# Scan stage: three token shifts spread over the slots of the inverse, and X's update signalled apart from its transpose's

## What is computed

```
z  = h @ w_in                                    # projection
z  = z[t-1]*w[0] + z[t]*w[1] + z[t+1]*w[2]       # centred_shift, three taps per channel
r, k, v, decays, rates = ...                     # from z, with sigmoids, a norm of k, exponentials
step(S):  s_kk = S kk ;  S <- S diag(d) - s_kk (kk*a)^T + v k^T ;  y = S r     # forward and reverse
```

## Time and profile before

| | us |
|---|---|
| median of 3 runs | 3002.47 (3000.74 to 3004.83) |
| profiled execution, its own time | 3004.26 |
| profiled execution, span | 3002.5 |
| PE busy over the span | 2732.5 (91%) |
| DVE busy | 1182.1 (39%) |
| ACT busy | 608.2 (20%) |
| POOL busy | 250.1 (8%) |
| mean granted TensorE clock | 0.974 of full speed |

### The profile page before, as it was taken

One profiled execution on the slowest core, in us unless ns is written; L12 is line 12 of the kernel. 1 busy time (PEld: TensorE's weight loads), 2 busy tenths in 40 slices (PEclk: granted clock), 3 DMA queues, 4 the chain that ended last, 5 costly groups with the idle time before them and its releaser, 6 DMA issues. The chain is left out here.

```text
span 3002.5 us, 69531 instructions
## 1 busy us (share of the span) xinstructions
PE 2732.5 (91%) x31106; PEld 1482.5 (49%) x31106; DVE 1182.1 (39%) x2613; ACT 608.2 (20%) x1255; POOL 250.1 (8%) x282
## 2 busy tenths in 40 slices
PE   6899999999999899988998989989887999899998
PEld 3566666776664445444433433433333455455553
DVE  3565566566643673163221211212013245423333
ACT  3233233333321100010000000000002344322222
POOL 1121122112200000001000000000000021110000
PEclk9999999999999999998999999999997999999999
DMA  5000000000005773167999999999995421042210
GB/s 204 24 26 14 19 26 20 21 19 26 12 26 196 279 282 113 56 273 297 430 431 431 430 431 430 431 431 430 431 431 196 134 71 37 0 123 63 63 42 29
DMA packets 191501, 557.42 MB, mean 186 GB/s; under 512 B 32140, under 2 KB 119714, under 8 KB 166646
## 3 DMA queue, kind: packets, MB, share of 16 engines
q1 hardware_dynamic: 191222, 553.19, 47.0%
HBM read 550.65 MB, written 2.24 MB: 184 GB/s over the span
## 5 line engine op out<-in xcount | busy, mean ns | idle before, releaser
L2327 PE MATMUL bank<-arena,xe 128*64 128x512 f32 x1024 | 345.2, 601 | 35.0 <-DMA gates<-in_exp_w_dram 24.0
L684 PE MATMUL bank<-arena 128*128 128x512 f32 x384 | 201.5, 647 | 6.7 <-DVE vj L1610 5.3
L2327 PEld LDWEIGHTS bank<-arena,xe 128*64 128x64 f32 x1024 | 107.9, 138 | 183.1 <-issue 170.4
L3354 PE MATMUL bank<-arena 128*128 128x512 f32 x384 | 176.2, 607 | 3.4 <-PEq L3232 3.4
L2327 PE MATMUL bank<-arena,hidT 128*64 128x512 f32 x512 | 171.7, 599 | 2.4 <-DMA gates<-in_exp_w_dram 1.9
L2780 PE MATMUL bank<-arena 128*128 128x512 f32 x320 | 143.3, 596 | 0.0
L2327 PE MATMUL bank<-mg_ring,xe 128*64 128x512 f32 x256 | 117.9, 615 | 20.9 <-DMA u<-in_exp_w_dram 20.9
L2552 DVE TENSOR_TENSOR x<-x,bank 128x512 f32<-128x512 f32 x64 | 43.7, 686 | 227.6 <-PE bank L2365 227.6
L2545 DVE TENSOR_TENSOR hid<-hid,bank 128x512 f32<-128x512 f32 x32 | 19.8, 682 | 285.4 <-PE bank L2327 285.4
L2327 PE MATMUL bank<-ys,xe 128*64 128x512 f32 x256 | 114.5, 600 | 19.1 <-DMA arena<-in_exp_w_dram 18.5
L1548 DVE TENSOR_TENSOR pm<-bank,m_level 128x512 f32<-128x512 f32 x120 | 82.7, 689 | 118.1 <-PE bank L763 117.1
(11 more groups left out here) (530 smaller groups left out, 5471.7 us busy)
## 6 DMA issues: line engine op xcount, KB each, us to landing
arena<-in_exp_w_dram SPq DMA_DIRECT2D x96, 2048.0 KB, 26.8
gates<-in_exp_w_dram SPq DMA_DIRECT2D x24, 2048.0 KB, 29.6
ys<-in_exp_w_dram SPq DMA_DIRECT2D x24, 2048.0 KB, 26.7
mg_ring<-in_exp_w_dram SPq DMA_DIRECT2D x24, 2048.0 KB, 25.7
u<-in_exp_w_dram SPq DMA_DIRECT2D x24, 2048.0 KB, 30.2
ws_w<-in_ada_w_dram SPq DMA_DIRECT2D x40, 1024.0 KB, 5.2
arena<-in_odd_w_in_dram SPq DMA_DIRECT2D x32, 512.0 KB, 3.9
arena<-in_w_in_dram SPq DMA_DIRECT2D x24, 512.0 KB, 4.2
```

The source lines that it names most:

```text
L684: last = mm(to[:], wj[:, c, i, :], hT[:, c, 0:T], start=(c == 0), stop=(c == KT - 1))
L2327: r[e] = mm(out[a, :], lhs[j][:, a], w[:, j, 512 * c:512 * c + 512], start=(first and j == 0), stop=(last and j == len(lhs) - 1), skip_gro ...
L3354: last = mm(o[:], w[:, i, t, :], hT[:, t, :], start=(t == 0), stop=(t == KT - 1))
```

## The change

The three shifts of K_X, K_V and R_X are taken apart into taps that stand in three successive places instead of one (V_X stays whole). The first two pieces of the projection R_X move on PE from (1,3,0), ahead of `solve`, to (1,3,1), behind `read_out`. `parts(j, 11)` moves on DVE from (1,3,0), ahead of `update`, to (1,3,1), behind `state`; `parts(b, 2)` from (2,2,1) to (2,3,0). X's update gets a semaphore of its own: for l > 0 the next product waits for that and no longer for XT's update, and a wait for XT's update stands between the product and the right side (levels 1 to 3). ACT's and POOL's programs are unchanged.

```diff
             def product_ready(j, g, l):
                 if l == 0:
                     sc.settled(pe, "x0", j, g)
-                if level_no(j, g, l) > 1:
+                if l:
+                    pe.wait_ge(S["x_first"], x_first_no(j, g, l - 1))
+                elif level_no(j, g, l) > 1:
                     pe.wait_ge(S["x_done"], level_no(j, g, l) - 1)
...
-                if at == (1, 3, 0):
+                if at == (1, 3, 1):
                     project(b, R_X, 0, KT)
                     project(b, R_X, 1, KT)
-                if at == (1, 3, 1):
                     squares(b)
...
                             product(j, s, l, sj, n + l - 1 if l else None, at_step)
+                        if l < 4 and live(j) and l:
+                            pe.wait_ge(S["x_done"], level_no(j, s, l - 1))
                         if l < 4 and s < 2:
                             right_side_beside_scores(sj, n + l, j, 4 + 4 * s + l)
...
-                    tt(x, x, z(INV), ALU.subtract)
+                    tt(x, x, z(INV), ALU.subtract).then_inc(S["x_first"], 1)
...
-            def shift(j, which):
+            def shift(j, which, taps=range(3)):
...
+                mine = Steps(dve, S["shift"], (shift_no(j, which - 1) if which else SHIFTED * j) + taps[0] * len(parts_))
+                if taps[0] == 0:
+                    dve.wait_ge(S["proj"], proj_no(j, which))
...
+                for tap in taps:
+                    if tap:
+                        mine.settle()
+                    for dst, z, w, n in parts_:
+                        if tap == 0:
+                            mine.then(ts(dst, z, w[1], None, ALU.mult))
+                        elif tap == 1:
+                            mine.then(stt(dst[:, 1:n], z[:, 0:n - 1], w[0], dst[:, 1:n], ALU.mult, ALU.add))
+                        else:
+                            mine.then(stt(dst[:, 0:n - 1], z[:, 1:n], w[2], dst[:, 0:n - 1], ALU.mult, ALU.add))
+                mine.settle()
...
             def beside(j, at):
                 a, b = j - 1, j + 1
-                if at[0] < 2 and at[1] < 4 and at[2] == 0:
+                if at[0] < 2 and at[1] < 4 and at[2] == (1 if at[0:2] == (1, 3) else 0):
                     parts(j, 4 + 4 * at[0] + at[1])
...
+                if at == (0, 2, 1):
+                    shift(b, K_X, (0,))
                 if at == (0, 3, 0):
-                    shift(b, K_X)
+                    shift(b, K_X, (1,))
+                if at == (0, 3, 1):
+                    shift(b, K_X, (2,))
...
+                if at == (1, 2, 0):
+                    shift(b, K_V, (0,))
                 if at == (1, 2, 1):
-                    shift(b, K_V)
+                    shift(b, K_V, (1,))
                 if at == (1, 3, 0):
+                    shift(b, K_V, (2,))
                     gated(a)
...
                 if at == (2, 2, 1):
                     parts(b, 0)
+                    shift(b, R_X, (0, 1))
+                if at == (2, 3, 0):
+                    shift(b, R_X, (2,))
                     parts(b, 2)
-                    shift(b, R_X)
```

More of the change, by code:

```diff
@@ L524, in stage_scan @@
     names = """p_loaded a2_loaded w2_loaded wk_loaded wr_loaded wv_loaded g_loaded zeroed ones_made summed grown q_grown r_grown
-        prod mask corr x_done part_moved xt0_done r_mm r_neg u_mm u_done z_mm z_done z_scaled y_mm y_copied
+        prod mask corr x_first x_done part_moved xt0_done r_mm r_neg u_mm u_done z_mm z_done z_scaled y_mm y_copied
         proj shift par_done sq_done ss_root ss_inv inverse_wide kk_done t1_done kf_done akk_done ke_done be_done q_done
@@ L595, in stage_scan @@
         level_no = lambda j, g, l: (j * GROUPS + g) * LEVELS + l + 1
+        x_first_no = lambda j, g, l: (j * GROUPS + g) * (LEVELS - 1) + l + 1
         step_no = lambda j, n: j * STEPS + n + 1
@@ L1585, in params @@
                     ts(col(j, 18), col(j, 10), -1.0, 1.0, ALU.mult, ALU.add).then_inc(S["par_done"], 1)
-            def shift(j, which):
+            def shift(j, which, taps=range(3)):
                 if not live(j):
                     return
-                dve.wait_ge(S["proj"], proj_no(j, which))
-                mine = Steps(dve, S["shift"], shift_no(j, which - 1) if which else SHIFTED * j)
-                taps_of = lambda i: [col(j, 3 * t + i) for t in range(3)]
+                w_of = lambda i: [col(j, 3 * t + i) for t in range(3)]
@@ L1594, in shift @@
                 z_of = proj_bank(j, which)
                 if which == K_X:
-                    if j:
+                    parts_ = ((kj[:, XS], z_of[:], w_of(1), T),)
+                elif which == K_V:
+                    parts_ = ((kj[:, CS], z_of[:, 0:TC], w_of(1), TC), (vj[:, CS], z_of[:, TC:2 * TC], w_of(2), TC))
+                elif which == R_X:
+                    parts_ = ((rj[:], z_of[:], w_of(0), T),)
+                else:
+                    parts_ = ((vj[:, XS], z_of[:], w_of(2), T),)
@@ L1597, in shift @@
+                mine = Steps(dve, S["shift"], (shift_no(j, which - 1) if which else SHIFTED * j) + taps[0] * len(parts_))
+                if taps[0] == 0:
+                    dve.wait_ge(S["proj"], proj_no(j, which))
+                    if which == K_X and j:
                         dve.wait_ge(S["ke_done"], 2 * j)
-                    shifted(mine, dve, [(kj[:, XS], z_of[:], T)], taps_of(1))
-                elif which == K_V:
-                    if j:
+                    if which == K_V and j:
@@ L1601, in shift @@
                         sc.settled(dve, "tokV", j - 1, 0)
[L1602 to L1615, removed]
+                    if which == V_X and j:
                         sc.settled(dve, "tokV", j - 1, 1)
                         sc.settled(dve, "tokV", j - 1, 2)
-                    shifted(mine, dve, [(vj[:, XS], z_of[:], T)], taps_of(2))
+                for tap in taps:
[6 more added lines that the diff above has]
+                            mine.then(stt(dst[:, 1:n], z[:, 0:n - 1], w[0], dst[:, 1:n], ALU.mult, ALU.add))
+                        else:
+                            mine.then(stt(dst[:, 0:n - 1], z[:, 1:n], w[2], dst[:, 0:n - 1], ALU.mult, ALU.add))
```

## The result

The changed kernel took 3019.56 us (median of 5, 3015.59 to 3026.71), the kernel before 3002.47: ratio 1.006, interval 1.0041 to 1.0078. It is **slower by 0.6%**.

The account below looks back on a forecast made before the run. PE, busy 740 of 800 us in the scan, was taken as the bound. Terms -1.5 - 1.0 + 9.0 + 2.1 + 3.3 = +12 us on the profiled 3004.26, less 1.8 to the median: 3014.5, range 3001 to 3023.

Parts of the forecast that it names:

- (0,3)/(0,4): Product of (0,4) loses its 0.81 us wait, but POOL limits the gain: 0.2 a turn, 1.5 us over seven turns.
- (1,3): Slot of the split K_V shift: solve 0.97 earlier, but projection then follows read-out uncovered, so next product 0.75 later.
- POOL's end: In (1,3)/(1,4), `parts(j, 11)` behind the state delays ACT's copies, then POOL, by 1.8 us, and (1,4)'s correction with it.
- The two slots together: (1,3) and (1,4): 5.3 in turns 4 to 6, 1.4 in turn 0, 2.2 in turns 1 to 3; together 9.0 us lost.
- (2,3): Mask 1.7 earlier, but ACT's copies wait for `parts(b, 2)` and block `solved`: read-out 0.3 later, x 7 = 2.1 us.
- The semaphore: Wins only at three products of turns 0 and 7, 0.33 each, together 1.0 us.
- twelve more waits a turn: Extra wait instructions on PE from the semaphore: taken as 0, at most 0.03 us each, 3 us in all.
- Turns 0 to 6 have a next turn, so seven is the count throughout: Count used for the terms per turn, in the (0,3)/(0,4) step; gives 0.2 x 7 turns = 1.5 us there.
- the clock's +3.3: Longer PE pauses in (1,3) bring 1.2 GHz stretches of 1.65 us cost; two in turns 1 to 3 counted, bounds 0 to 11.5.
- DVE's relief wins: Rival, chance 0.13: mask's 1.7 us in (2,3) reaches PE, and in (1,3) POOL does not bound; faster, 2993.5.
- The semaphore collects: Rival, chance 0.12: all 41 waits for XT shorten by 0.33, -13.5 in place of -1.0; no change, 3002.5.
- The clock stays up: Rival, chance 0.27: no clock term, +8.7 us, 3011; also where the skill's rule leads.

Follow-up runs that it names:

- K_V undone: Changed kernel with K_V's shift whole at (1,2,1), R_X's first two pieces and `parts(j, 11)` in their old places; 3010.97 us, 1.0017 to the kernel before.
- parts behind the tap: Changed kernel with `parts(j, 11)` back in (1,3,0), between K_V's last tap and gated; 3009.54 us, 1.0014 to the kernel before.
- the kernel with ACT's order: Changed kernel with `parts(j, 11)` ahead of the last tap, square behind `part_moved(j, 2)`, `part_moved(b, 0)` behind `solved`; 2974.16 us, 0.9893 to the kernel before.
- the semaphore alone: Kernel before with only the new semaphore added, all shifts, scores and projections where they were; 3009.84 us, 1.0010 to the kernel before.
- the second execution of the changed kernel: Changed kernel, unaltered, timed and profiled again beside other kernels; 3024.79 us, 1.0060 to the kernel before, span 3027.5.

## Why the forecast held, and where it did not

**Right by mechanism.** (0,3)/(0,4): forecast -0.2 a turn, measured -0.19 to -0.20 in turns 1 to 5. (1,3): solve 0.97 earlier, measured 0.90; the next product 0.75 later, measured 0.76 or 0.77. POOL's end 1.8 later, measured 1.98 (all three in turn 6, where the clock did not interfere). The two slots together: 9.0 forecast, 8.2 measured over turns 0 to 6. Inside that sum turns 1 to 3 were taken wrongly: not PE's own 0.75 was the bound there but POOL, whose end the correction follows by 0.07 us in all three; as the correction had come 1.1 to 2.5 us behind POOL before, after pauses of "issue" that are now waited out, the three turns together cost nothing (0.95 + 0.30 - 1.24), against 2.2 forecast. (2,3): +0.3, measured 0.29 or 0.30 in turns 0, 3 and 6; in turn 5 it was -0.20, because the read-out of the kernel before had come late there by itself, and in turns 1, 2 and 4 the clock differed. The semaphore: -1.0 forecast, nothing measurable in the times of two comparisons, 0.5 and 1.4 us in PE's idle time. The forecast counted twelve more waits a turn for it; the edit adds nine (levels 1 to 3 of three groups, 72 more in the trace), as the product's own wait is only exchanged for another. The copies' place on ACT, named there as what stands between the mask's 1.7 us and the read-out, is shown by the run that moved them.

**The step that failed** is the sentence "Turns 0 to 6 have a next turn, so seven is the count throughout". `parts(j, 11)` belongs to the turn itself, not to the next one, and moved in turn 7 too. That turn cost 4.8 us in the first profile, 3.5 of them in (1,4), and 8.9 in the second. The two kernels with `parts(j, 11)` ahead of the state again (K_V undone, parts behind the tap) are at 0.28 and 0.12 in that slot.

**The term that was mis-sized** is the clock's +3.3. PE's busy time in the scan rose by 6.4 us in one execution of the changed kernel and by 17.3 in the other, its idle time by 4.6 and 5.8 (forecast without the clock: 8.7). Where a slower matmul lies in time that would have been a wait, it costs nothing, so busy time is only an upper bound of the clock's price. In turns 0 to 6 the first execution lengthened the scan by only 5.1 us against the forecast's 12, the second by 12.3: the stretches fell elsewhere. So the sum came out 5 us under the median with two terms too low, turn 7 and the clock, and one too high, the idle time of turns 0 to 6. That it lies so near is in part luck: the errors offset each other, and one program's profiled executions spread by more than the whole forecast. The rule of the Trainium skill that the forecast weighed, page "TensorE: Matmul & The Clock Gate", section "HAM oscillation — how this bites in real kernels", by which these pauses would cost no clock, is not borne out: PE's pause of 1.82 us that ends at 584.67 is followed by 0.50, that is 1.2 GHz, from 585.2 us, and the kernel with ACT's order, which has no such pauses, has a mean clock of 0.977.

**The rivals.** "DVE's relief wins" fell for the reason given against it, and its gain in (2,3) came when that reason was taken away. "The semaphore collects" fell: the waits behind X are 10 us shorter in the list than those behind XT had been, but the semaphore alone took only 0.5 us off PE's idle time. "The clock stays up" fell: the scan's time at 1.2 GHz rose from 29.5 to 42.0 and 66.1 us.

What stays open: why one pause is followed by the lower clock and an equal one is not, how the 18 us of the K_V part divide between its waits and the clock, and what moving square alone would give.

## What to carry to other kernels

When work is taken off one engine's path, look in each slot for what stands in program order on the next engine between the freed result and its reader: here two steps of ACT and one of DVE, cheap where they stood, made the difference between a gain of 32 us and a loss of 17. Cover moved away (the projection ahead of solve) has to be moved together with what it covered (square, negate), in one edit. And count a moved step by whose index it carries: what belongs to this turn moves in the last turn too.

## What the chip showed that was not expected

Two executions of one program differed by 13.7 us of span, and most of it was the granted clock (0.972 and 0.968; 10.9 us of PE's busy time). Kernels whose pauses of 1.8 us were filled had 0.976 or 0.977 and gained more than the pauses' own length: of the 51 us of span between the second execution of the changed kernel and the best one, 24 are busy time of PE, that is the clock (13 of 37 us against the first execution). The semaphore kernel lost 1.2 to 1.7 us in (2,3) in turns 4 to 6 without a change there. As the stretches at 1.2 GHz lie in other slots even in two executions of one program, this need not come from its edit, and a difference of a few us between two kernels of this scan says little until the slots have been compared one by one.
